# Six of the memory's key tiles made inside the delta rule's second group, their norm one group sooner, and the output norm's factor as exp(-ln/2)

## What is computed

```python
def rwkv7_scan(r, w, k, v, kk, a):
    ...
    def step(state, inp):
        r_t, w_t, k_t, v_t, kk_t, a_t = inp
        sk = jnp.einsum('bhvk,bhk->bhv', state, kk_t)
        state = (state * w_t[:, :, None, :]
                 - sk[..., None] * (kk_t * a_t)[:, :, None, :]
                 + v_t[..., None] * k_t[:, :, None, :])
        y = jnp.einsum('bhvk,bhk->bhv', state, r_t)
        return state, y
...
    yr = rwkv7_scan(rr, w, kr, vr, kk, a)
    yr = (standardize_heads(yr, GN_EPS) * r_gn_g.astype(f32).reshape(R_HEADS, R_HDIM)
          + r_gn_b.astype(f32).reshape(R_HEADS, R_HDIM))
    yr = yr + jnp.sum(rr * kr * r_rk.astype(f32), -1, keepdims=True) * vr
    y_r = (yr.reshape(B, S, R_WIDTH) * g.astype(f32)).astype(h.dtype)
    return jnp.concatenate([y_m, y_r], -1) @ w_out
...
        memn = rmsnorm(mem, norm_mem[l])
        x = x + mem_cross_attn(h, memn, x_wq[l], x_wkv[l], x_wo[l])
```

## Time and profile before

| | us |
|---|---|
| median of 3 runs | 1660.65 |
| lowest, highest | 1659.09, 1663.93 |
| the profiled execution, time | 1663.44 |
| its span, first to last instruction | 1661.6 |
| PE busy | 1597.8 |

### The profile page before, as it was taken

The page is one execution under the profiler, slowest core; times in us unless marked ns, Lnnn a source line. Parts: engine busy times, 40 slices in busy tenths (PEclk is TensorE's granted clock), DMA queues, the critical chain, the costliest instruction groups (busy, mean ns, idle before and its releaser), DMA issues. The chain is left out here.

```text
span 1661.6 us, 25020 instructions
## 1 busy us (share of the span) xinstructions
PE 1597.8 (96%) x10298; PEld 1229.7 (74%) x10298; DVE 911.7 (55%) x1464; ACT 690.3 (42%) x1184; POOL 712.0 (43%) x357
## 2 busy tenths in 40 slices
PE   6999998879999899999999999999999999999999
PEld 5876666778887688888888888476676567787787
DVE  5957878446852427556531157697536663324251
ACT  5544454324432532222233234434645465455441
POOL 4533336234652145555564446343134422463342
PEclk9999999999999999999999999999999999999999
DMA  5321111003432032333333343022112210442132
GB/s 183 137 87 51 51 51 54 4 29 91 153 113 76 26 102 76 95 96 101 102 92 105 95 133 118 23 64 64 41 57 75 89 64 26 139 156 86 51 100 79
DMA packets 39713, 138.54 MB, mean 83 GB/s; under 512 B 4400, under 2 KB 5680, under 8 KB 38320
## 3 DMA queue, kind: packets, MB, share of 16 engines
q1 hardware_dynamic: 39600, 136.94, 26.1%
HBM read 132.73 MB, written 4.19 MB: 82 GB/s over the span
## 5 line engine op out<-in xcount | busy, mean ns | idle before, releaser
L396 POOL TENSOR_TENSOR parts<-ring,parts 128x1024 fp32r<-128x1024 f32 (+3 forms) x250 | 581.8, 2333 | 806.6 <-ACT parts L387 806.5
L435 PE MATMUL banks<-h_hi,parts 128*128 128x512 f32 x1120 | 461.9, 412 | 3.4 <-PEq L295 3.4
L437 PE MATMUL banks<-h_hi,parts 128*128 128x512 f32 x1120 | 438.1, 391 | 0.0
L436 PE MATMUL banks<-h_lo,parts 128*128 128x512 f32 x1120 | 437.6, 391 | 0.0
L387 ACT CAST parts<-ring 128x1024 fp32r<-128x1024 f32 (+3 forms) x251 | 244.8, 979 | 134.9 <-PE banks L437 134.8
L435 PEld LDWEIGHTS banks<-h_hi,parts 128*128 128x128 f32 x1120 | 211.4, 189 | 62.4 <-issue 18.7
L436 PEld LDWEIGHTS banks<-h_lo,parts 128*128 128x128 f32 x1120 | 211.5, 189 | 46.1 <-issue 5.1
L437 PEld LDWEIGHTS banks<-h_hi,parts 128*128 128x128 f32 x1120 | 210.9, 188 | 45.2
L3130 ACT CAST ffn_act_hi<-ffn_gate 128x512 fp32r<-128x512 f32 x22 | 13.7, 622 | 162.7 <-DVE ffn_gate L3029 162.7
L435 PE MATMUL banks<-ffn_act_hi,parts 128*128 128x512 f32 x176 | 68.5, 389 | 0.0
L436 PE MATMUL banks<-ffn_act_lo,parts 128*128 128x512 f32 x176 | 68.5, 389 | 0.0
(11 more groups left out here) (607 smaller groups left out, 2979.4 us busy)
## 6 DMA issues: line engine op xcount, KB each, us to landing
ring<-weights SPq DMA_DIRECT2D x211, 512.0 KB, 3.5
ring<-weights SPq DMA_DIRECT2D x24, 256.0 KB, 2.6
x<-xT SPq DMA_DIRECT2D x4, 1024.0 KB, 5.4
ring<-weights SPq DMA_DIRECT2D x8, 384.0 KB, 3.1
x_spill<-x SPq DMA_DIRECT2D x2, 1024.0 KB, 4.8
x<-x_spill SPq DMA_DIRECT2D x1, 2048.0 KB, 9.2
outT<-x SPq DMA_DIRECT2D x8, 256.0 KB, 2.0
ring<-weights SPq DMA_DIRECT2D x8, 192.0 KB, 2.4
```

The source lines that it names most:

```text
L396: self.nc.gpsimd.tensor_tensor(self.parts[:, t % PARTS, 1, 0:w], self.ring[:, t % SLOTS, 0:w], self.parts[:, t % PARTS, 0, 0:w].bitcast(F3 ...
L435: nc.tensor.matmul(out, w.hi, x.hi, start=first, stop=False)
L436: nc.tensor.matmul(out, w.hi, x.lo, start=False, stop=False)
L437: return nc.tensor.matmul(out, w.lo, x.hi, start=False, stop=last)
```

## The change

The key jobs leave the fill of the outputs and become a `Fill` of their own, `k.memory` (`memory_keys`), begun in the core. In group two each level has four of its steps behind the `cx` pair and four behind the `xcx` pair, and eight stand behind `wu`: six jobs of eight. The last two jobs (banks 2 and 3) stay in the outputs, eight steps first and eight in the first two state steps; the value jobs' steps are spread over the rest.

So that the normed memory is there in time, its turn comes at group one's last level, ACT copies the factor from PSUM to SBUF (`act_factor`, into the free `k.x[:, 3, MEM:S]`), and the norm's products, casts and low halves come at group one's end and group two's beginning. `memory_lo` now lies over `qk0`, which group one frees.

In the outputs the root and reciprocal become ACT's logarithm of variance + eps and, after all four, ACT's exponential of -0.5 times it; DVE's reciprocals go.

The diff, cut to what is used below (the rest are counters, an argument and tile positions):

```diff
@@ -995,33 +996,39 @@
+        dst, rows = self.tiles[i][4:6]
+        dve.wait_ge(*self.named("norm_high").ge(i + 1))
+        self.k.nc.vector.tensor_tensor(dst.lo, self.whole[0:rows, i % self.N, :], dst.hi.bitcast(F32),
+                                       ALU.subtract).then_inc(*self.named("low_dve").inc())
+    def act_factor(self, act):
+        act.wait_ge(*self.named("turned_ready").ge(1))
+        self.k.nc.scalar.copy(self.factor, self.k.banks[self.turn_bank][:, 0:self.n]).then_inc(*self.k.counter("gated_ready").inc())
...
@@ -1295,17 +1306,18 @@
                 raw = k.x[:, 4:8, :].rearrange("p a (b n) -> p (a b) n", n=MEM)
-                assert k.placed["lora_g"] == k.placed["gd"] + 2 * S * 4
-                mem = Halves(k.over("memory_hi", [P, DT, MEM], F32R, "x", 4 * S * 4), k.over("memory_lo", [P, DT, MEM], F32R, "gd"))
+                assert k.placed["gd"] == k.placed["qk0"] + 2 * S * 4
+                mem = Halves(k.over("memory_hi", [P, DT, MEM], F32R, "x", 4 * S * 4), k.over("memory_lo", [P, DT, MEM], F32R, "qk0"))
                 norm = Norms(k, ctx, [(D, [(raw[:, t, :], mem[:, t, :], P, k.vec("norm_mem", t)) for t in range(DT)])], MEM,
...
                              names=CORE_NORM, sum_bank=6, turn_bank=6)
+                norm.factor = k.x[:, 3, MEM:S]
+            value_ctx.close()
+            k.x_key = k.sbuf(x_ctx, "x_key", [P, DT, MEM])
             core = rwkv_core(k, [Pair(k, p, rkv, decay, values[p]) for p in range(PAIRS)], lanes, step_T, gain, gd, lora_g, rkv, norm)
             mlstm(k, h, normed, early, qk, v, o, rkv, wa, gd, lora, lora_g,
-                  [Operands(k, p, rkv, wa, lora, decay, values[p]) for p in range(PAIRS)], (e, topb, lowb, hm, u_col), core, raw, norm)
-            value_ctx.close()
+                  [Operands(k, p, rkv, wa, lora, decay, values[p]) for p in range(PAIRS)], (e, topb, lowb, hm, u_col), core, raw, norm, lambda: memory_keys(k, mem, norm))
             state = k.sbuf(ctx, "state", [P, NCH, PAIRS, CH], high=True)
-            k.x_key = k.sbuf(x_ctx, "x_key", [P, DT, MEM])
             k.x_value = k.sbuf(x_ctx, "x_value", [P, MEM // P, D])
@@ -1344,7 +1356,17 @@
-def mlstm(k, h_in, arriving, early, qk, v, o, rkv, wa, gd, lora, lora_g, pairs, rooms, core, raw, norm):
+CORE_JOBS, LEVEL_STEPS = 6, 4
+
+
+def memory_keys(k, mem, norm):
+
+    banks = (6, 7, 6, 7, 6, 5, 2, 3)
+    return Fill(k, [FeatureFill("x_k", mem, banks[t], "act", lambda e, c, b, t=t: k.nc.scalar.copy(k.x_key[:, t, :], b), MEM)
+                    for t in range(DT)], norm, apart=True)
+
+
+def mlstm(k, h_in, arriving, early, qk, v, o, rkv, wa, gd, lora, lora_g, pairs, rooms, core, raw, norm, memory):
@@ -1544,12 +1568,13 @@
             k.lora_landed = k.small_load()
-            k.prefetch(sp, k.used)
+            k.prefetch(sp, mixer_used)
...
             k.raw_landed = k.small_load()
+            k.prefetch(sp, mixer_used + CORE_JOBS)
@@ -2083,8 +2108,9 @@
                 pe.wait_ge(*norm.named("mean_ready").ge(1))
+                pe.wait_ge(*G("gated_ready").ge(1))
             else:
-                pe.wait_ge(*norm.named("whole_ready").ge(DT))
+                pe.wait_ge(*k.memory.taken(CORE_JOBS - 2))
         for e in range(2):
@@ -2096,6 +2122,8 @@
         pe.wait_ge(*C("wu_taken").ge(2 * g + 2))
+        if g and lane.lane:
+            pe.wait_ge(*k.memory.taken(CORE_JOBS - 1))
         beta, kappa, v = (lane.turned[:, i] for i in range(3))
@@ -2202,7 +2230,7 @@
         elif g:
-            pool.wait_ge(*lanes[1].count("part_ready").ge(n * g))
+            pool.wait_ge(*norm.named("norm_low").ge(DT // 4))
         else:
@@ -2256,19 +2288,28 @@
             pe.wait_ge(*other.count("z_taken").ge(g + 1))
+        if g:
+
+            pe.wait_ge(*G("output_taken").ge(PAIRS))
         for i in range(n):
...
                 pe_cx(pe, g, lane, i)
+            if g:
+                k.memory.pe(pe, LEVEL_STEPS)
             for lane, own in groups[g]:
                 pe_xcx(pe, g, lane, i)
+            if g:
+                k.memory.pe(pe, LEVEL_STEPS)
             if g == 0 and i == 2:
...
                 norm.pe_sums(pe)
-            if g and i == 0:
+            if g == 0 and i == n - 1:
                 norm.pe_turns(pe)
...
             pe_wu(pe, g, lane)
+        if g:
+            k.memory.pe(pe, DT)
         for lane, own in groups[g]:
@@ -2310,12 +2347,18 @@
                 norm.act_wide(act, 0, 1)
-            if g and i:
-
-                pe_free(act)
-                norm.act_parts(act, 2 * i - 2, 2 * i)
+                norm.act_factor(act)
+            if g:
+                k.memory.act(act, 2 * LEVEL_STEPS)
         for lane, own in groups[g]:
+            if g and lane.lane:
+                k.memory.act(act, DT)
             act_wu(act, g, lane)
+        if g == 0:
+            norm.act_parts(act, 0, DT // 2)
+        else:
+            k.memory.take(act, None, CORE_JOBS - 1)
+            k.memory.left = CORE_JOBS + 1
         for lane, own in groups[g]:
@@ -2323,6 +2366,7 @@
             if i == 0:
+                norm.act_parts(act, DT // 2)
                 act_gate(act, 2 * g)
@@ -2338,16 +2382,21 @@
                 norm.dve_rstd(dve)
-            if g and i < 4:
-                pe_free(dve)
-                norm.dve_parts(dve, 2 * i, 2 * i + 2)
+        if g == 0:
+            norm.dve_parts(dve, 0, DT // 2)
         for lane, own in groups[g]:
             dve_parts(dve, g, lane, own)
+        if g == 0:
+            norm.dve_parts(dve, DT // 2, DT, lows=False)
...
                 dve_masks(dve, g, i, step)
+        if g:
+            gates_read(dve)
+            for i in (DT // 2, DT // 2 + 2):
+                norm.dve_low(dve, i)
         dve_rest(dve, g)
@@ -2355,14 +2404,19 @@
                     pool_level(pool, g, lane, i)
+            if g and i == 0:
+                gates_read(pool)
+                norm.pool_parts(pool, DT // 2)
             if g == 0 and i < 2:
...
                 norm.pool_squares(pool, *NORM_TILES[i])
-            if g and i >= 2:
-                norm.pool_parts(pool, 2 * i - 4, 2 * i - 2)
+            if g and i:
+                k.split_low(pool, k.memory.first[i - 1] + 1 + LEAD)
         if g:
-            norm.pool_parts(pool, 2 * n - 4, DT)
+            k.split_low(pool, k.memory.first[CORE_JOBS])
+        else:
+            norm.pool_parts(pool, 0, DT // 2)
@@ -2383,11 +2437,10 @@
     square, y = query, [k.y[:, 4 + p, :] for p in range(PAIRS)]
-    fill = Fill(k, [FeatureFill("x_k", mem, 6 + t % 2 if t else 2, "act", lambda e, c, b, t=t: nc.scalar.copy(k.x_key[:, t, :], b), MEM)
-                    for t in range(DT)] +
-                [TokenFill("x_v", mem, MEM, banks, k.x_value[:, :, half * 512:(half + 1) * 512])
-                 for half, banks in enumerate(((6, 7), (4, 5)))])
-    FIRST_FILL, STEP_FILL = DT, 5
+    keys = k.memory
+    fill = Fill(k, [TokenFill("x_v", mem, MEM, (6, 7), k.x_value[:, :, half * 512:(half + 1) * 512]) for half in range(2)])
+    VALUE_STEPS = (0, 1, 3, 3, 3, 3, 3)
+    KEY_STEPS = (5, 3, 0, 0, 0, 0, 0)
     x_half = [slice(0, DT // 2), slice(DT // 2, DT)]
@@ -2427,17 +2480,18 @@
             pe.wait_ge(*G("part_copied0").ge(0))
-            fill.pe(pe, FIRST_FILL)
+            keys.pe(pe, DT)
...
                 pe_step(pe, c)
-                fill.pe(pe, STEP_FILL)
+                keys.pe(pe, KEY_STEPS[c])
+                fill.pe(pe, VALUE_STEPS[c])
...
             pe.wait_ge(*G("state_ready").ge(NCH))
-            pe.wait_ge(*fill.taken(0))
+            pe.wait_ge(*keys.taken(DT - 1))
             for p in range(PAIRS):
@@ -2459,14 +2513,20 @@
                 nc.scalar.copy(k.y_parts.hi[:, t, :], k.y[:, t, :]).then_inc(*G("high_made").inc())
-            fill.act(act, FIRST_FILL + STEP_FILL * (NCH - 1) + 2 * PAIRS)
+            keys.act(act, 2 * DT)
+            keys.take(act, None, DT - 1)
+            fill.act(act, sum(VALUE_STEPS) + 2 * PAIRS)
             for p in range(PAIRS):
...
                 nc.scalar.activation(square[p], y[p], ACT.Square).then_inc(*G("square_ready").inc())
+            fill.act(act, 4)
             for p in range(PAIRS):
-                fill.act(act, 4)
                 act.wait_ge(*G("sums_ready").ge(PAIRS + p + 1))
-                nc.scalar.activation(square[p], k.banks[p], ACT.Sqrt, bias=k.vec("gn_eps"), scale=1.0 / RHD).then_inc(*G("root_ready").inc())
+                nc.scalar.activation(square[p], k.banks[p], ACT.Ln, bias=k.vec("gn_eps"), scale=1.0 / RHD).then_inc(*G("ln_ready").inc())
+            fill.act(act, 4)
+            for p in range(PAIRS):
+                act.wait_ge(*G("ln_ready").ge(p + 1))
+                nc.scalar.activation(square[p], square[p], ACT.Exp, scale=-0.5).then_inc(*G("root_ready").inc())
             fill.end_act(act)
@@ -2494,7 +2554,6 @@
                 dve.wait_ge(*G("root_ready").ge(p + 1))
-                chain(nc.vector.reciprocal(square[p], square[p]))
```

51 lines of the change are left out of this document (28 added, 23 removed).

## The result

The changed kernel takes 1671.37 us (median of 6 runs, 1668.26 to 1675.37) against 1659.87 us (median of 6, 1657.46 to 1663.93) of the kernel before: ratio 1.0066, 95% interval 1.0046 to 1.0086. It is 0.7% slower, where 1658.5 and at most 1666 were forecast. Its profiled execution took 1668.26 us with a span of 1666.4; that is the fastest of its six runs, while the profiled one of before is among its slower ones, so the two traces are 4.8 us apart and the medians 11.5. Stretches of the traces tell where the time went, medians how much.

A forecast was written before the change was run, and what follows sets the result against it. It took the second group's 64x64 matmuls to be bound by instruction arrival. Terms: -4.0 (w_out 10.0 earlier, less 6.0 idle) + 0.3 + 1.5 = -2.2 us on 1660.65, so 1658.5; bounds 1655.7 to 1664, with rivals 1652.5 to 1666.

The forecast's parts named there:

- The diagnosis: Second group: its 64x64 matmuls use a block of instructions in 2.1 us, while one arrives each 3.7 us.
- Part 1: Key tiles moved into the second group: it takes 48.8 us instead of 41.0, +7.9, from +6 to +11.
- Part 2: Norm moved to group one's end and group two's beginning: +0.3 us (0 to 1); SyncE's moved loads cost nothing.
- The two waits that the part names: Second group: 0.9 us at level 0 for gate copy and mask, 1.2 us in wu for key tile 4's copy.
- Part 3: State chain and outputs: 45.9 us instead of 63.8, -17.9, with 2.4 us of gaps between state steps.
- The blocked chain: Rival, state steps 2 to 6: VectorE's addition waits for GpSimd's low halves, 11.5 us of gaps, 1667.6 us; chance 0.12.
- Part 4: Tail behind the last sum: first low half after 14.2 us, cover 8.2, so TensorE idles 6.0; clock loss adds 1.5.
- The clock: Behind the idle time at w_out: at most 3.4 us at half speed, +1.5 us, from 0 to 3.
- The gaps aren't instructions: Rival, second group: the four gaps laid to issue stay, 6.7 us, giving 1665.2 us; chance 0.09.
- My bound of +11: Second group's upper bound of growth, in us: the two gaps of 1.6 us in parts come again.
- if the group grows by more than 12: Sign against the forecast: second group longer by over 12 us (or by less than 6).
- distances between state steps is over 3.5 us: Sign against the forecast, state chain: state steps lie over 3.5 us apart.

The follow-up runs named there:

- e2: The changed kernel with the eight key steps between wu and parts put inside the first lane's parts; 1666.1 us, 1.0034 of the kernel before.
- e3: The changed kernel with the sixth weight tile and the x loads behind it asked for only after the second lane's parts are added; 1668.2 us, ratio 1.0042.
- e1: The changed kernel with w_out's first product waiting for the four logarithms instead of the exponentials; 1669.3 us, 1.0048 of the kernel before.
- e8: The kernel before with only the logarithms and exponentials in place of roots and reciprocals, first measurement; 1663.9 us, ratio 1.0023.
- e10: The kernel before with only the logarithms and exponentials, as e8, measured a second time; 1659.2 us, ratio 1.0006.
- e4: The changed kernel with square roots and VectorE reciprocals again instead of logarithms and exponentials; 1675.1 us, 1.0089 of the kernel before.
- e5: The changed kernel with w_out waiting for logarithms, one value step instead of two ahead of each sum and square, weight copies behind the exponentials; 1670.4 us, ratio 1.0056.
- e6: The changed kernel with e2's and e1's edits, one value step ahead of each sum and square, two weight copies left among squares and logarithms; 1663.2 us, 1.0021.
- e7: On top of e6: five key tiles instead of six in the second group, three steps instead of four per place; 1667.2 us, ratio 1.0048.
- e9: On top of e6: fifth key tile copied ahead of the first wu, GpSimd's w_out low half behind VectorE's low halves of y; 1659.5 us, ratio 1.0010.
- e11: On top of e9: three key tiles instead of six in the second group, five in the output stage; 1667.9 us, 1.0038 of the kernel before.
- e12: As e11 but with four key tiles in the second group and four in the output stage; 1665.1 us, 1.0017 of the kernel before.

## Why the prediction was wrong, step by step

**The diagnosis** held: the group is starved of instructions. What was wrong is the picture of how. I treated the blocks as a rate of one per 3.7 us on average, so that slow stretches would put blocks in store. e2 and e3 show that each block costs 3.7 us by itself when it is used up in 2.1: no slack of the levels is carried into parts. The packets say so too: between the one of 372.85 and the one of 385.85 us the changed kernel got none, though TensorE took 8.8 us (373.37 to 382.19) for the block ahead of the dense one.

**Part 1, +7.9 (bounds 6 to 11), was +17.4.** The step that failed reads "arrival no longer sets the pace, and blocks are ahead when parts starts; I take its two gaps away". A second one failed in part 2: "six tile loads come before x's first half, [...] its reader is 60 us later, so nothing". Of the 9.6 us that were missed:
- 3.8 us is the stall in parts. Of it 1.6 is what a dense block costs anyway. The other 2.2 are the transfers in it (e3): the sixth weight tile, asked for at 380.0 us, and x's first half, which is asked for at 380.4 us now and at 362.3 in the kernel before, where it had landed by 367.4, ahead of both stalls in parts. I had looked at its reader only, and not at what it holds up.
- About 3 us is half clock: the stretches at 335.6 and 388.1 above. The second goes with the stall (e2, e3). At most 1.7 us each; for the first the same level takes 9.0 us here and 7.8 in e2, where the clock was full.
- About 2 us is TensorE's own work, mis-sized. I gave the last level "half an xcx"; it has half the matmuls and the whole time:

```profile
370.07 2.08 PE L2095 MATMUL banks<-invT,tmpU 64*64 64x64 f32 x64
```

  That is 1.1 us. The three levels ahead of it take 7.26 us each, not 7.1 (0.5 together), and wu without its wait 3.9, not 3.35. Another 0.7 us is the first level, 7.8 us even at full clock. The two waits that the part names came as written: 1.0 us at the gate's copy (for 0.9 with the mask's), 1.1 at the key copy (for 1.2).

**Part 2, +0.3.** For x's load see above. The second group begins 0.7 us later than before in the two traces, but the half clock ahead of it differs by more than that; not resolved, and small.

**Part 3, -17.9, was -17.2.** The outputs take 46.7 us for a forecast 45.9, with waits of 1.3 and 0.4 us for the state (the forecast had 2.4 of gaps); the missing 1.6 us is in the pieces' own time. That the two misses partly cancel is luck. The blocked chain did not come: one state step lies 4.2 us after its predecessor, the others 2.6 to 2.9.

**Part 4, idle 6.0 and clock 1.5, was right in sum for a wrong reason.** From the last sum to the second halves were forecast 14.2 + 1.5 = 15.7 us; 15.4 were measured. But I had the 8.2 us of cover run under the tail and TensorE idle behind it. In fact w_out's first matmul names root_ready, which in the changed kernel is counted up by the exponentials, so the idle time stands in front and the cover behind, where VectorE's low halves ended beneath it:

```profile
452.42 4.75 DVE L1152 TENSOR_TENSOR y_parts_lo<-y,y_parts_hi 128x512 fp32r<-128x512 f32 x4
```

I had not read that wait in `queries`. e1 puts the idle time where I had it and gains nothing.

**The clock** was costed at one place only. In the five pieces the half clock rose from 3.4 to 13.6 us. Over the runs, (1 - mean granted clock) x span has a median of 16.7 us in the changed kernel's six runs and 8.3 us in the 23 runs of before beside e1. That is up to 8 of the 11.5 us (the clock is recorded to 0.001, so to 1.7 us). It is not a cost that can be added to the others: each of the three stretches in the changed kernel's five pieces stands at or just behind an idle time. In the pieces of the two traces the half clock is 10.2 us longer, at most 5.1 us of loss; whether the rest accounts for the 4 us that lie in no piece isn't shown.

**The rivals.** "The state chain is blocked" (1667.6) gave the nearest time, and didn't happen. "The gaps aren't instructions" (1665.2) is false. The truth was a fourth case: they are instructions, and stay. My bound of +11 had that ("the two gaps of 1.6 in parts again"), but not with a transfer in them, not with the clock. Of the signs that I named as proof against me, "if the group grows by more than 12" is the one that came, and one of the six distances between state steps is over 3.5 us.

## What to carry to other kernels

Small matmuls that use up a block of instructions faster than the next one comes cost the block's time, not their own; steps put elsewhere don't help them, and steps put among them were, over the whole stretch, still paid in full or nearly so. So work moved into such a stretch should be costed at its whole length, and loads kept out of it. A load that a change pushes back in its queue is to be costed where it lands now, even if its own reader is far off. And when a change gives a semaphore's last increment to a later instruction, look for everyone who waits for it, in the next stage too.

## What was not expected of the hardware

- A dense block of 256 instructions in parts took 3.5 to 4.0 us in quiet (before, e3, e8, e10) and 6.0 us while 1.5 MB of loads ran (after); its packet of instructions started where the last packet of the loads ended, at 385.85 us.
- Stalls of 3.6 to 3.8 us in parts came with 3.4 us at half clock in all four kernels that had them (after, e1, e4, e5). Where the stalls there were 1.9 us or less, none came in nine kernels (before, e2, e3, e6, e7, e9, e10, e11, e12) and one did in e8, from 377.3 us on, behind stalls of 1.3 and 1.9. So it is not a rule by length alone: stretches at half clock also stand at other places of every trace, the kernel before's included.
- A weight's low half on GpSimd made a 0.75 us product of VectorE last 2.7 to 3.0 us (e5, e6). The Trainium skill ("SBUF — State Buffer", "Who interferes with whom") says that a VectorE instruction with two SBUF inputs contends with GpSimd's reads, over a port pair that is locked by one of them at a time. The trace agrees: in e5 each of the three products began 0.4 to 0.6 us behind a low half and ended 0.5 us behind its end.
- Logarithm and exponential needed a table load each, 1.28 us (433.17 and 441.50 in the changed kernel):

```profile
433.17 1.28 ACT L2525 ACT_TABLE_LOAD   x1
...
441.50 1.28 ACT L2529 ACT_TABLE_LOAD   x1
```
